# Unread 128x512 products in front of the transposes' wait in the first 16 attention steps

## The reference

```python
def moba_attention(z, cos, sin):          # 4 heads, 64 wide, chunks of 128 queries
    ...
    p = jax.nn.softmax(sc, axis=-1).astype(v.dtype)
    ...
def mla_attention(z, g_q, g_kv, w_uq, w_ukv, cos, sin):
    ...
        sc = (jnp.einsum('bhqd,bhkd->bhqk', qn, k_nope)
              + jnp.einsum('bhqd,bkd->bhqk', qr, k_rope)).astype(jnp.float32) * scale
        sc = jnp.where(kpos[None, :] <= qpos[:, None], sc, NEG)
        p = jax.nn.softmax(sc, axis=-1).astype(v.dtype)
        return jnp.einsum('bhqk,bhkd->bhqd', p, v)

for l in range(DEPTH):                    # DEPTH = 2
    h = rmsnorm(x, norm_mix_pre[l])
    z = h @ w_in[l]
    ...                                   # two convolution groups, MoBA, MLA
    y = jnp.concatenate([y_a, y_b, y_c, y_d], axis=-1) @ w_out[l]
    x = x + rmsnorm(y, norm_mix_post[l])
    f = conv_ffn_block(rmsnorm(x, norm_ffn_pre[l]), w_ffn_up[l], conv_ffn[l], w_ffn_down[l])
    x = x + rmsnorm(f, norm_ffn_post[l])
```

## Time and profile before

| what | us |
|---|---|
| median of 3 runs | 1253.84 |
| the 3 runs | 1245.2, 1254.07, 1253.84 |
| profiled execution, its time | 1257.87 |
| profiled execution, span of the core | 1256.1 |
| PE busy in it | 1217.1 (97%) |
| mean granted TensorE clock | 0.970 |

### The profile page before, as it was taken

One profiled execution on the slowest core, in us unless ns is written; L12 is line 12 of the kernel. 1 busy time (PEld: TensorE's weight loads), 2 busy tenths in 40 slices (PEclk: granted clock), 3 DMA queues, 4 the chain that ended last, 5 costly groups with the idle time before them and its releaser, 6 DMA issues.

```text
span 1256.1 us, 15486 instructions
## 1 busy us (share of the span) xinstructions
PE 1217.1 (97%) x6006; PEld 1026.6 (82%) x6006; DVE 822.8 (66%) x1160; ACT 581.7 (46%) x879; POOL 208.7 (17%) x190
## 2 busy tenths in 40 slices
PE   6999999989999999999999999999899999999996
PEld 5888878878888888888898887888888888888885
DVE  4699647577666666544759976566776666665463
ACT  4465447454443444434445635555444444444432
POOL 1385136010000000000006823431000000000000
PEclk9999959999999999999999998699999999999999
DMA  8233212443333333456633333035233333336573
GB/s 241 80 85 94 78 41 85 155 130 101 101 94 92 100 101 101 151 196 211 196 98 84 84 94 85 17 130 172 83 111 94 101 101 90 95 101 198 172 229 121
DMA packets 157083, 147.36 MB, mean 117 GB/s; under 512 B 6831, under 2 KB 137811, under 8 KB 157011
## 3 DMA queue, kind: packets, MB, share of 16 engines
q1 hardware_dynamic: 156432, 145.64, 38.2%
q10 hardware_dynamic: 579, 0.74, 0.2%
HBM read 140.07 MB, written 2.10 MB: 113 GB/s over the span
## 4 chain that ended last, share of the span: by engine, by line
PE 88%; DVE 4%; POOL 4%; issue 1%; ACT 1%; DMA 1%; POOLq 0%; DVEq 0%; ACTq 0%
PE ps L508 28%; PE ps L510 28%; PE ps L509 28%; PE ps L733 2%; POOL cf_out L833 2%; POOL rms_r L824 1%; POOL prob L850 1%; PE ps L570 1%; DVE xn L924 1%; DMA rows<-in_vectors 1%; DVE wsp L415 1%; DVE yt L904 1%; PE ps L621 0%; PE ps L614 0%; DVE sm L1145 0%
## 5 line engine op out<-in xcount | busy, mean ns | idle before, releaser
L508 PE MATMUL ps<-xn,wsp 128*128 128x512 f32 (+2 forms) x1136 | 418.4, 368 | 12.1 <-DVE xn L924 12.1
L510 PE MATMUL ps<-xn,wsp 128*128 128x512 f32 (+2 forms) x1136 | 415.6, 366 | 0.0
L509 PE MATMUL ps<-xn,wsp 128*128 128x512 f32 (+2 forms) x1136 | 415.5, 366 | 0.0
L415 DVE TENSOR_TENSOR wsp<-raw,wsp 128x1024 fp32r<-128x1024 f32 (+1 forms) x250 | 311.2, 1247 | 156.2 <-ACT wsp L407 156.0
L407 ACT ACTIVATE wsp<-raw 128x1024 fp32r<-128x1024 f32 (+1 forms) x256 | 266.8, 1044 | 162.0 <-PE ps L510 129.4
L508 PEld LDWEIGHTS ps<-xn,wsp 128*128 128x128 f32 (+1 forms) x1136 | 214.6, 189 | 48.9 <-DVE xn L924 14.2
L510 PEld LDWEIGHTS ps<-xn,wsp 128*128 128x128 f32 (+1 forms) x1136 | 214.5, 189 | 35.3
L509 PEld LDWEIGHTS ps<-xn,wsp 128*128 128x128 f32 (+1 forms) x1136 | 214.6, 189 | 34.7 <-issue 0.5
L508 PE MATMUL ps<-wsp,hid 128*128 128x512 f32 (+1 forms) x488 | 189.7, 389 | 0.0
L510 PE MATMUL ps<-wsp,hid 128*128 128x512 f32 (+1 forms) x488 | 189.1, 387 | 0.0
L509 PE MATMUL ps<-wsp,hid 128*128 128x512 f32 (+1 forms) x488 | 189.0, 387 | 0.0
(11 more groups left out here) (145 smaller groups left out, 1339.7 us busy)
## 6 DMA issues: line engine op xcount, KB each, us to landing
raw<-in_w_ffn_up SPq DMA_DIRECT2D x88, 512.0 KB, 3.8
raw<-in_w_ffn_down SPq DMA_DIRECT2D x88, 512.0 KB, 4.0
raw<-in_w_in SPq DMA_DIRECT2D x40, 512.0 KB, 3.9
raw<-in_w_out SPq DMA_DIRECT2D x32, 512.0 KB, 3.4
x<-in_x SPq DMA_DIRECT2D x4, 512.0 KB, 8.3
xn<-xn SPq DMA_DIRECT2D x8, 256.0 KB, 3.2
out_x<-x SPq DMA_DIRECT2D x4, 512.0 KB, 4.1
xn<-kr SPq DMA_DIRECT2D x8, 128.0 KB, 3.1
```

Of the source, the lines that this page charges most:

```text
L415: eng.tensor_tensor(wsp[:, u % SPLIT, 1, 0:nk * n], raw[:, (l * NU + u) % RAW, 0:nk * n], fp(wsp[:, u % SPLIT, 0, 0:nk * n]), ALU.subtract ...
L508: pe.matmul(dst, a[0], b[0], start=start, stop=False, skip_group_check=True)
L509: pe.matmul(dst, a[0], b[1], start=False, stop=False, skip_group_check=True)
L510: return pe.matmul(dst, a[1], b[0], start=False, stop=stop, skip_group_check=True)
```

## The change

In step t, between `scores(t)` and `transposes(t - 3)`, PE gets two more products in steps 0 to 2 and one in steps 3 to 15; none from step 16 on. Each is one single matmul (not the three of a split product) of 128 rows, 128 output rows and 512 columns, of the high parts of MoBA's first query and key tiles, into bank 4. Nobody reads the result, it waits for nothing and signals nothing. That is 2*3 + 13 = 19 instructions (and 19 weight loads) in a layer, 38 in all.

```diff
+                def keep_clock():
+
+                    pe.matmul(ps[:, STAT, :], hid[:, QM, 0, 0:P], hid[:, KM, 0, :], start=True, stop=True,
+                              skip_group_check=True)
+
                 pe.wait_ge(qk_ready, l * 4 + 4)
                 for t in range(N_ATT + ATT_TAIL):
                     if t < N_ATT:
                         scores(t)
+                    for _ in range(2 if t < TRAIL else 1 if t < N_ATT // 2 else 0):
+                        keep_clock()
                     if TRAIL <= t < N_ATT + TRAIL:
                         transposes(t - TRAIL)
```

## The result

| | us | range of 7 executions |
|---|---|---|
| before | 1248.05 | 1244.54 to 1254.07 |
| with the change | 1241.98 | 1241.41 to 1242.32 |

The ratio is 0.9934, with a 95% interval of 0.9906 to 0.9962: 0.7% faster. That is inside the range given, but less than the 1% that the prediction called faster with 0.83, and 10.2 us above its likeliest value. It also lies above the forecast's own range, which ended at 1240.3; only the margin of some 2 us around it takes the result in. The executions also lie much closer together than before.

The account below looks back on a forecast made before the run. PE bounds the kernel, at half clock in the MoBA steps. Gains 0.2 + 9.25 + 1.7 and 0.4 + 9.25 + 1.2, together 22.0 us, take 1257.87 to 1235.9, less 4.0 gives 1231.8 us; own range 1226.6 to 1240.3, stated range 1225 to 1243.

Parts of the forecast that it names:

- That the clock is kept: Attention, both layers: added products hold clock 1.00 in every microsecond from 154 to 190 us; forecast chance 0.80.
- second rival: Attention: clock falls in both layers all the same, products can't help, 1267.0 us; chance 0.07.
- never earn it back: MoBA steps at half clock, being thin themselves, can't regain full clock; 34.1 us of layer 0 at 1.2 GHz.
- The start point: Whole program: gains taken from the profiled execution's 1257.87 us, then 4.0 taken off for the median of the runs.
- I take it as both layers fallen: Runs before: the median was read as having the clock down in both layers, despite one run at 1245.2 us.
- sum of gains: Steps 0 to 19, both layers: 11.15 and 10.85 us, together 22.0 us.
- The pace of MoBA steps: Steps 7 to 15: four steps in 6.8 us instead of 11.12, ends 6.1 and 7.3; gain 9.25 us a layer.
- my two ways: Four MoBA steps: half of 11.12 plus products, 6.47 us; or MLA steps plus products and row changes, 7.0 us.
- The start, steps 0 to 7: Scores of step 0 to step 7: 9.3 us in both layers, gain 0.2 and 0.4 us, ends 8.8 and 10.3.
- Steps 16 to 20: Scores of step 16 to step 20: 6.0 us with a wait for POOL up to 0.62; gain 1.7 and 1.2 us.
- first rival: Attention: the clock is kept in one layer only, the other pays for its products, 1249.4 us; chance 0.08.

Follow-up runs that it names:

- e5: Changed kernel with each added product on 32 rows of both operands instead of 128; 1281.08 to 1284.9 us in four executions, ratio 1.0288.
- e2: Changed kernel with only the two products in each of steps 0 to 2, none in steps 3 to 15; median 1251.18 us, ratio 0.9986.
- e7: Changed kernel (128 rows) with added products in steps 0 to 6 only, two in 0 to 2, one in 3 to 6; median 1235.37 us, ratio 0.9902.
- e6: Changed kernel with each added product on the 64 rows that its step's scores leave free; median 1234.58 us in ten executions, ratio 0.9917.
- e1: Kernel before, run once more without edit; 1243.58 to 1257.43 us in 12 executions, median 1248.6, ratio 1.0005.
- e3: Changed kernel without products in steps 0 to 2, one in each of steps 3 to 15; ten executions in three groups, the profiled one 1253.4 us.
- e9: As e8, with four products instead of one in step 6; median 1231.87 us in six executions, ratio 0.9867.
- e8: Changed kernel with products in steps 0 to 6 only, each on the 64 rows its step's scores leave free; median 1231.73 us, ratio 0.9894.
- e4: Changed kernel with each added product on 64 rows of both operands instead of 128; median 1238.13 us in four executions, ratio 0.9898.

## Why the prediction was right or wrong

**That the clock is kept: right.** All seven executions have a mean clock of 0.995 to 0.998, and the profile shows 1.00 through the attention. The reading behind it, that the rows in use count and not the busy share alone, holds: e5 changes only the rows and loses the clock every time. The plain form of the rule that spoke against the change (second rival) is refuted by it: PE busy for 30 of 30 us at 0.50. By that rule, which is in the Trainium skill's "TensorE: Matmul & The Clock Gate", section "What's actually happening", activity releases the throttle; the runs add that activity is not the profile's busy time. The start is where the clock has to be kept, but up to step 6 and not only to step 2 (e2, e7). That MoBA steps at half clock "never earn it back" is wrong as a rule: in e2 they did after 10 us, in e6 after 20.

**The start point: wrong, and the largest part of the miss in the gain (22.0 us forecast, 6.1 measured).** The step that failed is the one that takes the profiled execution's two full dips as what every execution has ("I take it as both layers fallen"). Their lengths differ from execution to execution (e1): 0.968 to 0.986. The gain from 1257.87 to 1241.49 was 16.4 us; measured on medians it is 6.1. The prediction even had the sign in hand, the one execution at 1245.2, and put it down as an exception. The same step costs 4.0 us in the forecast time: the median before was 4.0 below the profiled execution, and that was taken off the time after as well. But the 4.0 was a difference in half clock, and where the clock is kept there is none: the profiled execution after took 1241.49, the median is 1241.98. The 10.2 us above the likeliest value are, to rounding, these 4.0, another 0.5 between profiled execution and median, and the 5.6 by which the sum of gains is too high, taken apart below.

**The pace of MoBA steps: mis-sized.** "I take 6.8" for four steps, ends 6.1 and 7.3; measured 7.44, above the upper end. Two terms were small. Without products the steps take 6.33 at full clock (e2), not half of 11.12 = 5.56, though PE has no wait in them: the gaps where the rows change don't halve. From scores to transposes, PE is late by 0.12 us against its pace at half clock (164.81 to 165.36 in the profile before, less 0.43) and by 0.09 at full clock (165.90 to 166.22 in e2, less 0.23); the row of the profile before stands below. And a product costs 0.28 in that place, 0.23 and part of a change; MLA steps plus 8 x 0.1 + 0.91 gave 7.0, the better of my two ways. Over steps 7 to 16 that is 16.12 instead of 14.7, 1.4 us a layer.

```profile
165.36 0.47 PE L733 MATMUL ps<-ident,prob 128*128 128x128 f32 x1
```

**The start, steps 0 to 7: mis-sized.** 10.03 instead of 9.3. The seven products up to step 4 add 1.8 us (5.16 against 3.36), though the pause of 0.73 is gone. PE has no wait at all from step 0 to step 7 after the change, so this is PE's own work and no late chain: a pair takes 0.66 us (155.81 to 156.47) where the sum had 0.45, and the changes of rows around it were counted five times at 0.1 for the whole start, too few. e6 confirms it from the other side: beside the scores, the same number adds nothing.

**Steps 16 to 20: right**, 6.03 for 6.0, with the wait of 0.66 for POOL that was expected in layer 0.

**What goes unpredicted elsewhere: 1.3 us**, 1.1 of it ahead of the attention (below) and so not an effect of the products. From 22.0 to 16.4: 2.8 in steps 7 to 16 of both layers, 1.5 in their starts, 1.3 elsewhere. The ends of the prediction's range are summed 0.2 us a layer too wide (2.4 and 2.0 are what its terms give, not 2.6 and 2.2), which changes nothing here. The first rival, one layer only, did not come up in seven executions; it does in the profiles of e2, e3 and e6, where products are fewer or have fewer rows.

**What the products themselves cost.** The changed kernel keeps the clock and lies 10.1 us above e9 (1231.87), where the products are nearly free. In the profiles 7.7 us of that are in the attention (32.18 and 32.19 from step 0 to 20, against 28.32 and 28.36), and these are the price of products in line. The rest lies before the first scores (1.5 us) and behind the attention, where both do the same work; it is no price of the products. Before, the median execution lost about 15 us to the clock (1246 to 1248 against 1232, or 0.017 of mean clock at 9.3 us for each 0.01); the change wins that and gives about half of it back in products that run in line.

## What to carry to other kernels

A stretch at half clock in one profile is one draw: look at the mean clock of several executions before you price it, and expect a fix to narrow the spread as much as it moves the median. Work that only keeps the clock up belongs where the clock is lost (here seven steps of 32) and on rows that its neighbours leave free. There it started beside them and cost next to nothing; in line it cost 0.28 us a product. Trimming has a price in certainty: a fall in one execution of six (e8) or three of ten (e6) can stay hidden in a short series.

## What the runs showed of the hardware

- Two products on different 64-row halves run side by side, even if they stand three instructions apart: starts 177.69 and 177.70 (e4), and four steps in 6.55 instead of 7.08 us. The Trainium skill, "TensorE: Matmul & The Clock Gate", section "Why this matters for your kernels", says the same of small-K products on distinct row groups; the trace agrees.
- The clock came down (1.00 to 0.50 at 156.8) with PE busy all the time since the first scores, when products used 32 and 64 rows, and stayed at 1.00 with the same columns at 128 rows (e5 against the change).
- The 64-row MoBA steps held full clock from step 7 on in e7, won it back after 10 us in e2 and 20 us in e6, and didn't in 34 us of the kernel before.
- The recorded clock can be wrong near the start of a trace. From 20 to 22 us the profile after says 1.00, and PE issues 11 instructions; before, at 1.00, it was 19 in the same stretch of the same work. Table of stretches, after and then before:

```profile
20.00:22.00 2.00, 2.00 (x11) 2.00 (x11) 2.00 (x3) 1.00 (x1) 0.00 (x0) 1.00 1.09 265
```

```profile
20.00:22.00 2.00, 2.00 (x19) 2.00 (x18) 2.00 (x2) 0.83 (x1) 0.00 (x0) 1.00 1.06 259
```

The pace says half clock. The work before is the same in both kernels, so when the clock first comes up differs from execution to execution; most of the 1.1 us by which the first attention began later is lost there.
